# A four-stage layer kernel: first stage built from token rows, head 0 of the delta stage and its out gate reordered, a second weight buffer in the mLSTM stage, weights split inside the branch operand of the last stage

## The chip, the cores and the metric

One core of a Trainium2 chip. The metric is the time of one execution on the device in microseconds (us). Runs of this kernel agree within about 0.2%.

## The reference

One layer for 1,024 prompt tokens and 8 sequences of 8 sample tokens (1,088 tokens, model width 1,024), all in float32.

```python
h = rmsnorm(x, g_mix)
proj = h @ w_in        # q_a k_a v_a i f o_a | qkv_b a_b beta_b z_b | gate_a gate_b
ha = mlstm(q_a, k_a, v_a, i, f) ...            # 4 heads
hb = gated_delta(conv(qkv_b), a_b, beta_b) * silu(z_b)   # 8 heads
mix = sigmoid(gate_a) * (ha @ w_pa) + sigmoid(gate_b) * (hb @ w_pb)
x = x + mix @ w_out
x = x + square(relu(rmsnorm(x, g_ffn) @ w_up)) @ w_down
x = x + sigmoid(rmsnorm(x, g_ple) @ w_pg) * (p @ w_pp)
y = rmsnorm(x, g_final)
```

## The kernel before, in words

Every large product is made exact enough from two rounded parts: an operand is split into a high part (rounded) and a low part (what is left), and a product is three matmuls, low x high, high x low, high x high. A weight slab is 1,024 x 128. SP loads it into a raw buffer, VectorE (DVE) writes its high part (`split_hi`, line 211, tile `w_hi`), GpSimd (POOL) its low part (`split_lo`, line 216, tile `w_lo`), and TensorE (PE) makes 72 matmuls of it: 8 row tiles x 3 matmuls x 3 groups of tokens (384, 384, 320 columns; `product`, line 227). The high and low buffers are double; the raw buffer is single, so the next load waits for `split_lo`. Each engine runs a list written out by hand, with semaphore waits, and there is a barrier between the four stages:

1. `prologue`: loads x by token rows in three pieces, turns it on PE (line 409), squares and sums it over features with a product by ones (line 396), scales it on DVE (line 480), splits it into `hhi` and `hlo` [all 8 row tiles], and stores the turned x (`XT`) to memory.
2. `delta`, tiles `b_*`: first the `gates` part (a product with 24 gate columns of `w_in`, line 616, then a chain of scans and exponentials on DVE and ScalarE (ACT); its rows go to memory as `ROWS_B` and `ROWS_A` and come back to all partitions), woven into the first turn of head 0; then a loop over heads 1 to 6, and head 7. In a turn PE makes the projections K, Q, V, Z of coming heads between the small products of the delta rule. K of the next head is projected in the turn of a head. `out_gate` (line 1581) is DVE's last step of the head before, on what PE turned into two banks (line 1125).
3. `mlstm`, tiles `a_*`: four heads, six slabs each (K, Q, VA, VB, OA, OB), the previous head's output stored to `HA` between the loads of OA and OB on SP's queue. ACT issues loads and stores of the states.
4. `tail`, tiles `t_*`: twice a branch (A, then B): two gate slabs as products with `hhi`/`hlo`, while the branch operand (`HA` or `HB`, 4 loads into `t_rraw`) is split by `branch` into `t_rhi` and `t_rlo`: 8 tiles, high parts and the low parts of odd tiles on DVE, low parts of even tiles on POOL; then the first branch product runs tile by tile (`product_by_tile`, line 239). After that `w_out`, the feed-forward blocks, the last gate and the output.

The order of first use in head 0 is given twice: in the engines' lists (`first_turn`) and in `early`, which assigns PSUM banks.

Of the kernel before, what the change touches and what calls it, by code (L numbers as in the profile page):

```python
# [26 lines left out]
P = 128  # L27
D = 1024
# [217 lines left out]
def build(nc, x_prompt, x_sample, p_prompt, p_sample, state_C, state_n, state_m, state_S, state_conv, g_mix, w_in,  # L246
# [38 lines left out]
    with ctx:  # L285
# [25 lines left out]

        def prologue():
            with ExitStack() as st:
                sb = sbuf_in(st)
                xrow = sb("xrow", [P, NCH, D])
                xT = sb("xT", [P, KT, T])
                sq = [sb(f"sq{i}", [P, KT, 384]) for i in range(2)]
                rb = [sb(f"rb{g}", [P, 384]) for g in range(NG)]
                hf = sb("hf", [P, KT, 384])
                gm = sb("gm", [P, KT])  # L320
                crow = sb("crow", [28, 3 * H_B * P])
                s_x = [sem(f"x_landed{i}") for i in range(3)]
                s_gm, s_small = sem("gm_landed"), sem("small_landed")
                s_const = sem("const_ready")
                s_tr = [sem("x_turned_even"), sem("x_turned_odd")]
                s_cpy = [sem("x_copied_act"), sem("x_copied_dve")]
                s_sq, s_ss, s_ln, s_rs = sem("x_squared"), sem("x_summed"), sem("x_log"), sem("x_rms")
                s_hf, s_hhi, s_hlo = sem("h_made"), sem("h_hi"), sem("h_lo")
                s_out = sem("xT_stored")
                s_ct, s_ctc = sem("conv_turned"), sem("conv_copied")  # L330
                def hf_of(g):

                    return (hf, sq[0], sq[1])[g][:, :, 0:GROUPS[g][1]]

                def turned(eng, half, c, copy):
                    w = L if c < NC else NB * NS
                    eng.wait_ge(s_tr[half], c + 1)
                    src = psum[(2 * c + half) % 6][:].rearrange("p (k t) -> p k t", k=4)[:, :, 0:w]
                    copy(xT[:, 4 * half:4 * half + 4, c * L:c * L + w], src).then_inc(s_cpy[half], 1)

                with nc.Block() as block:
                    @block.sync
                    def _(sp):
# [5 lines left out]
                        sp.dma_start(gm[:], g_mix[0].rearrange("(k p) -> p k", p=P)).then_inc(s_gm, 16)  # L349
                        sp.dma_start(crow[0:24, :], state_conv[0].rearrange("b j c -> (b j) c")).then_inc(s_small, 16)  # L350
                        sp.dma_start(crow[24:28, :], conv_w[0]).then_inc(s_small, 16)
                        sp.wait_ge(s_cpy[0], NCH)
# [5 lines left out]
                    def _(pool):  # L358
# [9 lines left out]
                                           pattern=[[-1, P]], channel_multiplier=1).then_inc(s_const, 1)  # L368
                        pool.affine_select(out=madd[:], in_=madd[:], compare_op=ALU.is_ge, fill=NEG, base=0,
# [13 lines left out]
                        for g in range(2):  # L383
                            a, w = GROUPS[g]
                            pool.wait_ge(s_hhi, g + 1)
                            pool.tensor_tensor(hlo[:, :, a:a + w], hf_of(g), hhi[:, :, a:a + w], ALU.subtract).then_inc(s_hlo, 1)

                    @block.tensor
                    def _(pe):
                        def sums(g):  # L390
                            w = GROUPS[g][1]
                            pe.wait_ge(s_sq, g + 1)
                            if g >= 2:
                                pe.wait_ge(s_ln, g - 1)
                            for k in range(KT):
                                ins = pe.matmul(psum[6 + g % 2][:, 0:w], ones[:], sq[g % 2][:, k, 0:w], start=(k == 0),
                                                stop=(k == KT - 1))
                            ins.then_inc(s_ss, 1)

                        pe.wait_ge(s_const, 7)  # L400
                        for c in range(NCH):
                            w = L if c < NC else NB * NS
                            if c % 3 == 0:
                                pe.wait_ge(s_x[c // 3], 16 if c < 6 else 32)
                            for half in range(2):
                                if c >= 3:
                                    pe.wait_ge(s_cpy[half], c - 2)
                                for k in range(4):
                                    ins = pe.transpose(psum[(2 * c + half) % 6][:, k * P:k * P + w],
                                                       xrow[0:w, c, (4 * half + k) * P:(4 * half + k + 1) * P],  # L410
                                                       ident[0:w, 0:w])
                                ins.then_inc(s_tr[half], 1)
                            if c in (4, 6):
                                sums(c // 2 - 2)
                        sums(2)
# [3 lines left out]
                        for i in range(3 * H_B):  # L419
                            ins = pe.transpose(psum[i // 12][:, 28 * (i % 12):28 * (i % 12) + 28],  # L420
# [5 lines left out]
                    def _(act):  # L426
# [3 lines left out]
                        def squares(g):  # L430
                            a, w = GROUPS[g]
                            act.wait_ge(s_cpy[0], 3 * g + 3)
                            act.wait_ge(s_cpy[1], 3 * g + 3)
                            if g >= 2:
                                act.wait_ge(s_ss, g - 1)
                            act.activation(sq[g % 2][:, :, 0:w], xT[:, :, a:a + w], ACT.Square).then_inc(s_sq, 1)

                        def logs(g):
                            w = GROUPS[g][1]
                            act.wait_ge(s_ss, g + 1)  # L440
                            act.activation(rb[g][:, 0:w], psum[6 + g % 2][:, 0:w], ACT.Ln, scale=1.0 / D, bias=eps[:]).then_inc(s_ln, 1)

                        def exps(g):
                            w = GROUPS[g][1]
                            act.wait_ge(s_ln, g + 1)
                            act.activation(rb[g][:, 0:w], rb[g][:, 0:w], ACT.Exp, scale=-0.5).then_inc(s_rs, 1)

                        def high(g):
                            a, w = GROUPS[g]
                            act.wait_ge(s_hf, KT * (g + 1))  # L450
                            act.activation(hhi[:, :, a:a + w], hf_of(g), ACT.Copy).then_inc(s_hhi, 1)

                        act.wait_ge(s_const, 11)
                        for c in range(3):
                            turned(act, 0, c, copy)
                        squares(0)
                        for c in range(3, 6):
                            turned(act, 0, c, copy)
                        squares(1)
                        logs(0)  # L460
                        exps(0)
                        for c in range(6, NCH):
                            turned(act, 0, c, copy)
                        squares(2)
                        logs(1)
                        logs(2)
                        exps(1)
                        exps(2)
                        for g in range(NG):
                            high(g)  # L470

                    @block.vector
                    def _(dve):
                        def scaled(g):
                            a, w = GROUPS[g]
                            dve.wait_ge(s_rs, g + 1)
                            if g:
# [2487 lines left out]
```

## Time and profile before

| | before |
|---|---|
| median of 3 runs | 2828.61 us (2827.95 to 2834.41) |
| profiled execution, its own time | 2830.69 us |
| its span | 2829.0 us |
| PE, DVE, ACT, POOL busy | 92%, 41%, 23%, 22% |
| mean granted TensorE clock | 0.963 of full speed |

The span runs from the first to the last instruction; the execution's own time is 1.7 us longer. Times in rows are counted from the span's start. Stage 1 lasts to about 68, stage 2 to about 927, stage 3 to about 1383.

### The profile page before, as it was taken

What the parts mean: (1) busy time and instruction counts of PE and PEld (TensorE: products, weight loads), DVE (VectorE), ACT (ScalarE), POOL (GpSimd) and SP (SyncE); (2) the same over time, 40 slices, a digit from 0 to 9 for tenths busy, and PEclk for the clock granted to TensorE, in tenths of its full rate; (3) what the DMA queues carried; (4) which work ended last, traced back from release to release, by engine and by line L of the source; (5) the groups of instructions that cost most, each with busy time, mean ns of one, the idle gap of its engine ahead of it and who ended that gap; (6) DMA issues with size and microseconds to landing.
All of it is one profiled execution on the core that took longest, in us unless ns stands there. A gap on an engine that the chain in (4) does not pass through costs nothing.

```text
span 2829.0 us, 40488 instructions
## 1 busy us (share of the span) xinstructions
PE 2615.4 (92%) x16191; PEld 2542.3 (90%) x16191; DVE 1168.1 (41%) x1930; ACT 645.5 (23%) x1322; POOL 636.1 (22%) x321
## 2 busy tenths in 40 slices
PE   3779999999998799999589999999999999999997
PEld 2769999999997799998489999999999999999897
DVE  4565556556544143453421312654223123134534
ACT  4535454545444111111100000011001000010112
POOL 2332121221210111110122321442212212212421
PEclk7889999999999899999799999999999999999998
DMA  3131221122201316523611211211111111111211
GB/s 131 27 94 43 63 71 54 40 70 63 63 9 31 94 39 95 86 48 53 123 45 44 101 45 44 101 45 45 45 45 45 45 39 52 45 38 45 68 35 67
DMA packets 235322, 165.33 MB, mean 58 GB/s; under 512 B 23211, under 2 KB 222443, under 8 KB 235151
## 3 DMA queue, kind: packets, MB, share of 16 engines
q1 hardware_dynamic: 217414, 154.69, 19.7%
q10 hardware_dynamic: 17792, 8.95, 2.3%
q8 instruction: 90, 1.47, 0.2%
q14 instruction: 26, 0.21, 0.0%
HBM read 135.84 MB, written 27.76 MB: 58 GB/s over the span
## 4 chain that ended last, share of the span: by engine, by line
PE 46%; DVE 2%; issue 1%; DMA 1%; POOL 1%; ACT 0%; POOLq 0%; DVEq 0%; ACTq 0%
PE bank L227 41%; PE bank L239 4%; PE bank L2609 1%; DVE t_rlo L2745 0%; DMA t_w_raw<-in_w_in_dram 0%; PE bank L2646 0%; POOL t_w_lo L216 0%; DVE t_rhi L2742 0%; DVE hlo L2771 0%; DVE hhi L2768 0%; POOL t_rlo L2457 0%; DMA t_rraw<-HB 0%; PE bank L2521 0%; DVE hraw L2915 0%; DVE t_x L2837 0%
## 5 line engine op out<-in xcount | busy, mean ns | idle before, releaser
L216 POOL TENSOR_TENSOR t_w_lo<-t_w_raw,t_w_hi 128x1024 fp32r<-128x1024 f32 x112 | 270.0, 2411 | 953.1 <-DVE t_w_hi L211 953.1
L227 PE MATMUL bank<-t_rlo,t_w_hi 128*128 128x384 f32 (+1 forms) x1248 | 409.5, 328 | 4.6 <-issue 4.6
L227 PE MATMUL bank<-t_rhi,t_w_lo 128*128 128x384 f32 (+1 forms) x1248 | 409.4, 328 | 2.5 <-issue 2.5
L227 PE MATMUL bank<-t_rhi,t_w_hi 128*128 128x384 f32 (+1 forms) x1248 | 409.2, 328 | 0.0
L227 PE MATMUL bank<-hhi,t_w_lo 128*128 128x384 f32 (+1 forms) x1224 | 399.6, 327 | 2.5 <-POOL t_w_lo L216 2.5
L227 PE MATMUL bank<-hhi,t_w_hi 128*128 128x384 f32 (+1 forms) x1224 | 399.7, 327 | 0.0
L227 PE MATMUL bank<-hlo,t_w_hi 128*128 128x384 f32 (+1 forms) x1224 | 399.5, 326 | 0.0
L227 PE MATMUL bank<-hhi,b_w_lo 128*128 128x384 f32 (+1 forms) x768 | 272.1, 354 | 11.4 <-POOL b_w_lo L216 11.4
L227 PE MATMUL bank<-hhi,b_w_hi 128*128 128x384 f32 (+1 forms) x768 | 253.8, 330 | 0.0
L227 PE MATMUL bank<-hlo,b_w_hi 128*128 128x384 f32 (+1 forms) x768 | 253.5, 330 | 0.0
L227 PEld LDWEIGHTS bank<-t_rlo,t_w_hi 128*128 128x128 f32 x1248 | 236.1, 189 | 5.2 <-issue 5.1
L227 PEld LDWEIGHTS bank<-t_rhi,t_w_lo 128*128 128x128 f32 x1248 | 236.0, 189 | 3.1 <-issue 2.9
L227 PEld LDWEIGHTS bank<-t_rhi,t_w_hi 128*128 128x128 f32 x1248 | 236.1, 189 | 0.0
L227 PEld LDWEIGHTS bank<-hhi,t_w_lo 128*128 128x128 f32 x1224 | 230.2, 188 | 3.0 <-POOL t_w_lo L216 3.0
L227 PE MATMUL bank<-hhi,a_w_lo 128*128 128x384 f32 (+1 forms) x576 | 205.5, 357 | 28.2 <-POOL a_w_lo L216 26.7
L227 PEld LDWEIGHTS bank<-hhi,t_w_hi 128*128 128x128 f32 x1224 | 230.2, 188 | 0.0
L227 PEld LDWEIGHTS bank<-hlo,t_w_hi 128*128 128x128 f32 x1224 | 230.1, 188 | 0.0
L2792 DVE TENSOR_TENSOR t_x<-t_x,bank 128x384 f32<-128x384 f32 (+1 forms) x120 | 62.7, 530 | 317.5 <-PE bank L227 276.4
L227 PE MATMUL bank<-hlo,a_w_hi 128*128 128x384 f32 (+1 forms) x576 | 191.9, 333 | 0.0
L227 PE MATMUL bank<-hhi,a_w_hi 128*128 128x384 f32 (+1 forms) x576 | 191.6, 333 | 0.0
L2704 ACT ACTIVATE t_acc<-t_v 128x384 f32<-128x384 f32 (+1 forms) x96 | 48.5, 507 | 614.1 <-DVE t_v L2812 614.1
L211 DVE CAST t_w_hi<-t_w_raw 128x1024 fp32r<-128x1024 f32 x112 | 107.5, 959 | 188.1 <-PE bank L227 132.9
(377 smaller groups left out, 4346.2 us busy)
## 6 DMA issues: line engine op xcount, KB each, us to landing
b_w_raw<-in_w_in_dram SPq DMA_DIRECT2D x32, 512.0 KB, 4.0
t_w_raw<-in_w_up_dram SPq DMA_DIRECT2D x32, 512.0 KB, 3.9
t_w_raw<-in_w_down_dram SPq DMA_DIRECT2D x32, 512.0 KB, 3.9
a_w_raw<-in_w_in_dram SPq DMA_DIRECT2D x24, 512.0 KB
t_w_raw<-in_w_in_dram SPq DMA_DIRECT2D x16, 512.0 KB, 3.7
b_gam<-ROWS_B SPq DMA_DIRECT2D x8, 576.0 KB, 5.0
b_kb<-ROWS_B SPq DMA_DIRECT2D x8, 576.0 KB, 3.6
b_eg<-ROWS_B SPq DMA_DIRECT2D x8, 576.0 KB, 3.5
```

The costliest lines, as they stand in the source:

```text
L211: dve.tensor_copy(self.hi[j % 2][:, 0:kt, :], self.raw[j % self.rs][:, 0:kt, :]).then_inc(self.hi_done, 1)
L216: pool.tensor_tensor(self.lo[j % 2][:, 0:kt, :], self.raw[j % self.rs][:, 0:kt, :], self.hi[j % 2][:, 0:kt, :], ALU.subtract).then_inc(sel ...
L227: ins = pe.matmul(out, a[:, k, :], b[:, k, :], start=(start and k == 0 and i == 0), stop=(stop and k == kt - 1 and i == 2))
L239: ins = pe.matmul(out, x[:, k, :], y[:, k, a:a + w], start=(k == 0 and i == 0), stop=(k == KT - 1 and i == 2))
L2609: ins = pe.matmul(bank[:, 0:w], x[:, k, m * P:m * P + P], v[:, k, a:a + w], start=(k == 0 and i == 0), stop=(k == 1 and i == 2))
L2704: act.activation(ACC[:, a:a + w], V[:, a:a + w], ACT.Square).then_inc(rsq.sem, 1)
L2792: B.release(dve.tensor_tensor(XM[:, m, a:a + w], XM[:, m, a:a + w], src[:, 0:w], ALU.add), ("dense", j, g))
```

## The change

It has six parts.

(1) The first stage works by rows. ACT squares each chunk of 128 tokens, DVE sums it per token, ACT takes the root, DVE the reciprocal, and a diagonal matrix of the reciprocals is the moving operand of a float32 product whose stationary operand is the chunk of x: it turns and scales at once. ACT writes `hhi` from PSUM with the gain as scale, DVE `hlo`. The plain transposes for `XT` stay, between these products.

(2) The gate weights are loaded and split in the first stage. The first load of the delta stage is head 0's K slab, and the memsets for the gate stand in another order.

(3) Head 0: two groups of V stand ahead of the norm of K, Z ahead of K of head 1, and the loads and splits follow.

(4) In the loop `out_gate` stands ahead of the split of the next head's Q.

(5) The mLSTM stage has two raw buffers.

(6) In `branch` the split of the first branch slab stands after four of the eight tiles, on DVE and POOL.

```diff
+                        def scaled(g, k):
+                            n = KT * g + k
+                            if n >= 6:
+                                pe.wait_ge(s_hlo, n - 5)
+                            for i, c in enumerate(chunks_of(g)):
+                                w = rows(c)
+                                if k == 0:
+                                    pe.wait_ge(s_dg, c + 1)
+                                ins = pe.matmul(psum[n % 6][:, L * i:L * i + w], xrow[0:w, c, k * P:k * P + P],
+                                                DG[0:w, c, 0:w], start=True, stop=True)
+                            ins.then_inc(s_h, 1)
...
+                            act.activation(hhi[:, k, a:a + w], psum[n % 6][:, 0:w], ACT.Copy, scale=gm[:, k:k + 1]).then_inc(s_hhi, 1)
...
+                            dve.scalar_tensor_tensor(hlo[:, k, a:a + w], psum[n % 6][:, 0:w], gm[:, k:k + 1],
+                                                     hhi[:, k, a:a + w], ALU.mult, ALU.subtract).then_inc(s_hlo, 1)
...
                 def product(pe):
-                    pe.wait_ge(s_lo, 1)
...
-            early = dense(Q_) + dense(V_) + normed(Q_) + dense(K_)[:1] + thirds("p1") + dense(K_)[1:] + [("rep", 0), ("rep", 1)]
-            early += dense(Z_) + thirds("e0", "kt", "p2", "vt")
+            early = dense(Q_) + dense(V_) + dense(Z_)[:2] + normed(Q_) + thirds("p1") + dense(Z_)[2:] + dense(K_)[:2]
+            early += [("rep", 0), ("rep", 1)] + dense(K_)[2:] + thirds("e0", "kt", "p2", "vt")
...
+                        slab(0, K_, 0, 0)
                         gate.loads(sp)
-                        slab(0, K_, 0, 0)
...
                         slab(0, V_, 2, 0)
+                        slab(0, Z_, 3, 0)
                         gate.stores(sp)
                         for i in (0, 2, 1):
                             row(0, i)
-                        slab(0, K_, 3, 1)
                         sp.wait_ge(gate.done, 1)
                         samples(0)
                         wait(sp, dx, 0, 3)
                         row(1, 0)
                         read(sp, 0, ("p1", 2))
                         row(1, 2)
-                        slab(0, Z_, 4, 0)
+                        slab(0, K_, 4, 1)
                         slab(1, Q_, 1, 1)
...
-                WS = Weights(sb, sem, "a_w", per=NJ)
+                WS = Weights(sb, sem, "a_w", per=NJ, raw_slots=2)
...
-                        def branch(i):
+                        def branch(i, s):
                             for k in range(KT):
+                                if k == KT // 2:
+                                    WS.split_hi(dve, s, 0, B)
                                 if k % 2 == 0:
```

On DVE, in head 0, this stood before around the three thirds of `p1` that `lower` reads (`b_at`), up to the small blocks `b_d` for PE's `replicated` product:

```order
L1519 SCALAR_TENSOR_TENSOR b_dt<-b_gam,b_hg,madds 128x128
L1540 TENSOR_TENSOR b_kb<-b_k,b_kb 128x1152
L1594 TENSOR_TENSOR b_at<-bank,b_dt 128x384 x3
L1530 SCALAR_TENSOR_TENSOR b_cv<-b_xp,b_taps,b_cv 128x1112 x3
L1511 COPY b_taps<-CT 128x84
L1600 TENSOR_TENSOR b_d<-b_at,b_bm 128x1152
```

and this stands there now:

```order
L1565 SCALAR_TENSOR_TENSOR b_dt<-b_gam,b_hg,madds 128x128
L1586 TENSOR_TENSOR b_kb<-b_k,b_kb 128x1152
L211 CAST b_w_hi<-b_w_raw 128x1024
L1640 TENSOR_TENSOR b_at<-bank,b_dt 128x384 x3
L1576 SCALAR_TENSOR_TENSOR b_cv<-b_xp,b_taps,b_cv 128x1112 x3
L1557 COPY b_taps<-CT 128x84
L1646 TENSOR_TENSOR b_d<-b_at,b_bm 128x1152
```

The high part of the fifth slab (K of head 1, whose load stands on SP behind a wait for `p1`) now comes ahead of `lower`.

On DVE in the loop over heads, around `out_gate` (`b_kd<-bank,b_gbh,b_z`), before and then now:

```order
L211 CAST b_w_hi<-b_w_raw 128x1024
L139 REGISTER_ALU
L1581 SCALAR_TENSOR_TENSOR b_kd<-bank,b_gbh,b_z 128x384
L139 REGISTER_ALU
L1581 SCALAR_TENSOR_TENSOR b_kd<-bank,b_gbh,b_z 128x384
```

```order
L1627 SCALAR_TENSOR_TENSOR b_kd<-bank,b_gbh,b_z 128x384
L139 REGISTER_ALU
L1627 SCALAR_TENSOR_TENSOR b_kd<-bank,b_gbh,b_z 128x384
L139 REGISTER_ALU
L1627 SCALAR_TENSOR_TENSOR b_kd<-bank,b_gbh,b_z 128x320
L204 ISA
L139 REGISTER_ALU
L211 CAST b_w_hi<-b_w_raw 128x1024
```

The split went behind the three steps of `out_gate`.

On DVE at the start of the last stage (branch A), now:

```order
L211 CAST t_w_hi<-t_w_raw 128x1024 x2
L2793 CAST t_rhi<-t_rraw 128x1088 x2
L2796 TENSOR_TENSOR t_rlo<-t_rraw,t_rhi 128x1088
L2793 CAST t_rhi<-t_rraw 128x1088 x2
L2796 TENSOR_TENSOR t_rlo<-t_rraw,t_rhi 128x1088
L211 CAST t_w_hi<-t_w_raw 128x1024
L2793 CAST t_rhi<-t_rraw 128x1088 x2
L2796 TENSOR_TENSOR t_rlo<-t_rraw,t_rhi 128x1088
```

Before, the third `t_w_hi` followed the eighth `t_rhi` and the fourth `t_rlo`; POOL's `t_w_lo` moved in the same way.

## Rows read from the trace of the kernel before

**Rows 1.** What PE waited for: us in total, times, longest us.
```profile
PE bank L616 <- DVE gw_lo L677: 33.3, 1, 33.3
PE bank L227 <- POOL a_w_lo L216: 26.7, 4, 14.0
...
PE bank L239 <- POOL t_w_lo L216: 16.4, 3, 9.4
PE bank L227 <- POOL b_w_lo L216: 11.4, 2, 10.8
PE bank L1125 <- DVE b_kd L1581: 10.8, 7, 1.7
...
PE bank L1079 <- ACT b_v L1308: 8.7, 1, 8.7
```

**Rows 2.** Timeline of the first stage: start, us, engine, line, out<-in, count, [idle before <-releaser].
```profile
7.47 6.40 PE L409 MATMUL bank<-ident,xrow 128*128 128x128 f32 x40 [7.47 <-DMA xrow<-in_x_prompt_dram]
...
12.94 2.77 ACT L436 ACTIVATE sq<-xT 128x3072 f32<-128x3072 f32 x1 [0.63 <-DVE xT L339]
...
33.19 0.40 SPq L354 DMA_DIRECT2D XT<-xT  x1
...
68.50 0.10 POOL L588 MEMSET g_bias<- 128x1 f32 x1 [3.50 <-POOLq L262]
...
76.48 0.69 PE L616 MATMUL bank<-hhi,gw_lo 128*128 128x384 f32 x1 [33.27 <-DVE gw_lo L677]
```

**Rows 3.** DMA issues: engine, count, KB each, median us from issue to landing.
```profile
b_w_raw<-in_w_in_dram SPq DMA_DIRECT2D x32, 512.0 KB, 4.0
...
XT<-xT SPq DMA_DIRECT2D x1, 4352.0 KB, 12.3
```

**Rows 4.** Busy time in two stretches: window, us, engines, PEclk, DMA share, GB/s.
```profile
7.50:35.00 27.50, 20.48 (x104) 15.36 (x104) 7.71 (x13) 17.01 (x17) 0.00 (x0) 1.00 0.37 120
1092.60:1099.00 6.40, 6.33 (x27) 6.30 (x28) 0.69 (x1) 0.02 (x1) 1.50 (x1) 0.68 0.76 214
```

**Rows 5.** Timeline of PE: float32 products of 128 columns.
```profile
288.30 2.17 PE L1138 MATMUL bank<-b_q,b_k 128*128 128x128 f32 x18
```

**Rows 6.** Timeline of head 0's first turn, DVE and PE.
```profile
152.08 0.69 DVE L211 CAST b_w_hi<-b_w_raw 128x1024 fp32r<-128x1024 f32 x1 [17.99 <-DMA b_w_raw<-in_w_in_dram]
...
155.24 0.69 PE L227 MATMUL bank<-hhi,b_w_lo 128*128 128x384 f32 x1 [10.75 <-POOL b_w_lo L216]
...
177.85 2.40 PE L1154 MATMUL bank<-b_d,b_bo 128*128 128x512 f32 x4 [5.63 <-DVE b_d L1608]
```

**Rows 7.** Timeline of the loop's first turn, and of head 7.
```profile
280.42 1.77 DVE L211 CAST b_w_hi<-b_w_raw 128x1024 fp32r<-128x1024 f32 x1 [1.69 <-PE bank L227]
...
282.27 2.40 POOL L216 TENSOR_TENSOR b_w_lo<-b_w_raw,b_w_hi 128x1024 fp32r<-128x1024 f32 x1 [0.63 <-DVE b_w_hi L211]
...
322.48 0.42 PE L227 MATMUL bank<-hhi,b_w_lo 128*128 128x384 f32 x1
...
863.22 0.55 PE L1125 MATMUL bank<-ident,b_kbe 128*128 128x128 f32 x3 [0.38 <-DVE b_kd L1581]
```

**Rows 8.** Timeline of the mLSTM stage around head 1's OA slab.
```profile
1063.60 0.60 ACTq L2112 DMA_DIRECT2D out_dram<-a_cs  x1
...
1089.43 0.69 DVE L211 CAST a_w_hi<-a_w_raw 128x1024 fp32r<-128x1024 f32 x1 [12.77 <-DMA a_w_raw<-in_w_in_dram]
```

**Rows 9.** The chain that ended last: start, us, what, count.
```profile
1425.92 14.63 PE bank L239 x72
...
1622.27 13.80 PE bank L239 x72
...
2177.07 12.01 PE bank L239 x72
```

**Rows 10.** Timeline of the last stage's two branch operands.
```profile
1413.20 1.35 DVE L2742 CAST t_rhi<-t_rraw 128x1088 fp32r<-128x1088 f32 x2
...
1622.27 0.65 PE L239 MATMUL bank<-t_rhi,t_w_lo 128*128 128x384 f32 x1 [3.83 <-POOL t_w_lo L216]
```

More of the change, by code:

```diff
@@ L454, in _, with raws @@
+                        def raws(c):
+                            for half in range(2):
+                                if half == 0 or not on_vector(c):
+                                    raw_copy(act, half, c, copy)
+                        act.dma_start(gm[:], g_mix[0].rearrange("(k p) -> p k", p=P)).then_inc(s_gm, 16)
+                        act.wait_ge(s_const, 7)
                         for c in range(3):
-                            turned(act, 0, c, copy)
-                        squares(0)
+                            square(c)
+                            raws(c)
@@ L457, in _ @@
+                        root(0)
                         for c in range(3, 6):
[L458 to L468, printed above, removed]
@@ L469, in _ @@
-                        for g in range(NG):
-                            high(g)
+                            square(c)
+                        act.wait_ge(s_gm, 16)
+                        for g in range(NG):
+                            for k in range(KT):
+                                if g < NG - 1 and k in (2, 4, 6):
+                                    raws(3 * g + 2 + k // 2)
+                                high(g, k)
+                            if g < NG - 1:
+                                root(g + 1)
+                            if g == 0:
+                                for c in range(6, NCH):
+                                    square(c)
+                            if g == 1:
+                                act.wait_ge(s_w, 64)
+                                act.activation(GWH[:], gwr[:], ACT.Copy).then_inc(s_gh, 1)
@@ new lines, in _ @@
+                        raw_copy(dve, 1, 2, dve.tensor_copy)
+                        diagonals(0)
+                        for c in range(3, 6):
+                            reduce(c)
+                        dve.wait_ge(s_gm, 16)
+                        for g in range(NG):
+                            for k in range(KT):
+                                if g < NG - 1 and k == 6:
+                                    raw_copy(dve, 1, 3 * g + 5, dve.tensor_copy)
+                                low(g, k)
+                            if g < NG - 1:
+                                diagonals(g + 1)
+                            if g == 0:
+                                for c in range(6, NCH):
+                                    reduce(c)
@@ L1211, in first_turn @@
                                 whole(0, Q_, g, 0, 1)
+                            for g in range(2):
+                                whole(0, V_, g, 0, 2)
                             pe.wait_ge(s_mask, MASKS)
@@ L1216, in first_turn @@
                                 taken(pe, -1, ("dense", K_, g))
-                            for g in range(NG):
-                                whole(0, V_, g, 0, 2)
+                            whole(0, V_, 2, 0, 2)
                             for g in range(NG):
@@ L1468, in first_turn @@
                             exps(-2, K_)
+                            gate.columns(act)
                             silu(0, Q_, QN)
@@ L1474, in first_turn @@
                                 copy_out(0, V_, g)
-                            gate.columns(act)
                             first_tap(0, 0, V_)
+                            for g in range(2):
+                                z_gate(0, g, False)
                             decays(0)
@@ L1736, in rest @@
                             masks(h)
-                        gate.weights(dve)
                         WS.split_hi(dve, 0, 0, FB)
```

263 lines of the change are left out of this document (134 added, 129 removed).

## The prediction

> **What bounds the kernel now.** I first read the page's busy shares: PE is the engine that is nearly always at work, so the time is PE's work plus PE's waits, and an edit is worth what it takes out of those waits. Next come PE's waits by what ended them [rows 1]: the gate weights of the second stage (33.3 us, once), the mLSTM stage's low weights (26.7 in four, of which 14.0 is that stage's start and stays), the last stage's low weights (16.4 in three), head 0's low weights (11.4) and norm (8.7), and the out gate of the loop (10.8 in seven). Then I read the stretches one by one in the timeline. The first stage hands over at 68.50, and PE stands idle until 76.48 [rows 2], because the second stage begins by zeroing, loading and splitting the gate weights. In head 0 DVE waits 17.99 us for a slab whose load was queued behind the gate rows, and PE waits for that slab and then for DVE [rows 6]. In the loop DVE first waits for PE, then splits, and only then does the out gate [rows 7]. In the mLSTM stage DVE waits 12.77 us for the OA slab to land, which shares the DMA engines with the state stores issued at 1063.60 [rows 8]. In the last stage the wait ends with POOL's low part, which comes after the whole branch operand [rows 10].
>
> A stall costs more than its length: the granted clock falls behind it. In the stretch after the OA wait it averaged 0.68 [rows 4], that is partly 1.2 and partly 2.4 GHz; 72 products took 14.63 and 13.80 after the two branch stalls against 12.01 undisturbed [rows 9].
>
> **The change part by part.**
>
> *Last stage.* Without the stall at branch A, 9.4 [rows 1] and 14.63 - 12.01 = 2.6 [rows 9] go; at branch B 3.83 [rows 10] and 13.80 - 12.01 = 1.8. Sum 17.6. The third wait of that group (16.4 - 9.4 - 3.8 = 3.2) is at the mix operand and stays. Is the slab ready in time? DVE reaches the fifth tile at 1413.20 [rows 10]; the split takes 0.7 (152.08 row [rows 6]) and POOL 2.4 [rows 7], so the low part ends at about 1416.3. PE ends its gate slabs at 1425.92 - 9.4 = 1416.5. That is tight, but a miss would cost only its own length. The operand's later tiles come 0.7 later on DVE and 2.4 later on POOL; PE needs one each 12.01 / 8 = 1.5 us, the eighth at 1427, and DVE has it by about 1424. I take 17.6; the bounds are 12 (a new small wait in each branch) and 17.6.
>
> *mLSTM stage.* Three waits of 26.7 - 14.0 = 12.7 in all [rows 1] are for OA. With two raw buffers its load no longer waits for VB's low part but for VA's, one slab earlier, so it is issued before the state stores at 1063.60 [rows 8] instead of among them. The clock: at a mean of 0.68 over 6.4 us [rows 4], 6.4 x 0.32 = 2.0 is lost; for three about 5. Sum 17.5. What is late next: OB's load now stands behind the two stores to `HA` and is issued while the states are still being written; its split stands on DVE ahead of the steps that free PE's banks. In the old order OA landed at 1089.4 [rows 8] and the bytes in flight are the same, so OB should land near 1091. PE was ready for OA at about 1088 (the split at 1089.43 [rows 8], 0.7 for it and 2.4 on POOL make 1092.5, less a wait of 12.7 / 3 = 4.2), and with OA there it needs DVE for a bank one group later (4.2, a third and a bit of 12.01), at 1092. Bounds: 5 (that wait eats most of it) and 17.5.
>
> *Loop.* Each of six turns loses 1.7 at `out_gate` [rows 1]. Head 7 has no split there and loses 0.38 [rows 7]; that is the same code with the split taken away. The six lose (10.8 - 0.38) / 6 = 1.73 each, so (1.73 - 0.38) x 6 = 8. The split it is moved behind feeds Q of the next head: its low part begins at 282.27, ends at 284.7, and PE uses it at 322.48 [rows 7], so 2 us of delay are covered by 37.8. Bounds 0 and 9.
>
> *Gate wait.* 76.48 - 68.50 = 8.0 [rows 2] becomes about 0.5. But DVE's list has the split of Q ahead of the gate's further steps, and Q's load now waits on K's low part, which waits on POOL's memsets; I count 1 lost. Term 6.5, bounds 5 and 8.
>
> *First stage.* x's first piece lands at 7.5 [rows 2]. Squares of 3,072 columns take 2.77 [rows 2], so a chunk takes 1.0. Three squares, five copies out of PSUM (0.55 each, estimated from that rate), a table load, the root and the diagonals: the first scaled product starts at about 17. A float32 pass of 128 columns costs 2.17 / 18 = 0.12 [rows 5], two passes for a product; per group of 384 tokens PE makes 24 products and 24 transposes, (48 + 24) x 0.12 = 8.7. ACT has eight scaled copies (0.45 each, estimated as above), five plain ones and, in the first group, three squares: 9.5. So each group takes some 9.5, the groups end near 27, 37 and 44, and the split of the gate weights and the copies of the conv columns end at 47. `XT`, issued at 33.19 before [rows 2], is issued at about 36 when the last plain copy is out, and its landing takes 12.3 [rows 3]: 48.5, which ends the stage. With the barrier the next begins at 50 instead of 68.50. Term 18.5. Bounds: 22 (copies faster) and 3 (PE at 1.2 GHz, below). The old work removed (sums, logarithms, the large splits) lay in this stretch and is in the difference of its ends.
>
> The granted clock in this stretch was 1.00 from 7.5 to 35, with PE busy 20.48 of 27.5, on transposes and float32 products mixed [rows 4]. The Trainium skill, page "TensorE: Matmul & The Clock Gate", section "Part 4: PE-mode transpose", says that transposes do not count as PE activity in the way products do; by that the first stage, a third transposes, could run at the low level, and the term would be 3 instead of 18.5. By the row it is 18.5, and I go with the row.
>
> *Head 0.* V's first two groups fill the 8.7 wait of the norm [rows 1], so the gate rows leave earlier, and DVE's wait of 17.99 [rows 6] goes, because Z is loaded ahead of the rows. That moves DVE's tables 18 earlier. Given back: PE now makes two groups of Z ahead of `p1` and waits for Z's weights, +5. Then a new wait: SP loads K of head 1 only after `p1`, with a row ahead of it, and DVE splits it ahead of `lower`: 4.0 of landing [rows 3], some 1.5 for the row and 0.7 for the split, +6.5; behind it on POOL the low part (2.4) stands ahead of the diagonal steps of `b_at`, +1.8. So the replicated product, at 177.85 before [rows 6], gains only 18 - 13.3 = 5. Behind it stood 12.01 of Z [rows 9]; now a third of K remains, and DVE's convolution can follow, which returns about 6. Sum 11; PE's shorter stalls in here bring the low clock into the substitution's small products, and I take 2 off: 9. Bounds 0 and 16.
>
> Edits that I put at nothing: ACT's queue for the gain vector and the memsets' order, hidden behind x's landing and the gate product.
>
> **Sum.** 17.6 + 17.5 + 8 + 6.5 + 18.5 + 9 = 77. The profiled execution took 2830.69, so 2753.6; the median of the runs is 2.1 lower, which makes 2752. About 0.3% is what a measurement of this kernel can tell from no change, 8 us.
>
> **The rivals.**
>
> *The first stage runs at 1.2 GHz.* Passes take 0.24, a group 17, the stage ends near 65: 2752 + 15.5 = 2767. Against it stands the 1.00 of [rows 4]; for it the long wait for x and the serial start. Chance 0.1.
>
> *Head 0 gains nothing.* DVE's wait for K of head 1 and slow small products take all nine: 2761. For it: the load stands behind `p1`. Chance 0.12.
>
> *OB takes OA's place* in the mLSTM stage: if it lands at 1096 or later, DVE holds PE for about 4 in each of three heads: 2764. For it: a store to `HA` ahead in the queue. Chance 0.1.
>
> *Better:* PE keeps 2.4 GHz in head 0 and ACT's copies are quicker: 2738 to 2742. Chance 0.1.
>
> *Slower.* One mechanism could do it: the split moved behind `out_gate` feeds every turn of the loop. It starts to cost when it is more than 37.8 late [rows 7], and to undo 77 us over six turns it would have to be 37.8 + 13 = 51 late in each, with PE idle 13 a turn: 2830 or more. DVE's move is 2. Chance 0.02.
>
> *The change does not do what it says:* PE turns out to be bound elsewhere and the waits reappear one for one, 2825 to 2830. Against it: after each of these stalls PE runs on without another wait for a hundred products or more. Chance 0.02.
>
> **How the numbers follow.** The forecast, 2752, has 0.54. The cases with one rival reach 2767; two together would be 2773. The better case reaches 2738. That range holds 8 in 10 or a bit more. Faster 0.96, same 0.02, slower 0.02.
>
> **What would show it.** Right: the second stage's first instruction near 50, its gate product within 1 of that; no PE wait for OA, and none for the first branch slabs; PE's wait at the out gate below 0.5 in each turn; in head 0 DVE waiting about 10 for the fifth slab ahead of `b_at`. Wrong: a granted clock of 0.5 between 15 and 45; `XT` landing after 55; DVE waiting for OB's landing past 1093 of the old count; Z or K of head 1 holding PE for more than 6.

## The result, and the profile after

The changed kernel takes 2750.96 us (median of 4 runs, 2746.87 to 2752.34), the kernel before 2830.27 beside it (4 runs, 2827.95 to 2834.41): a ratio of 0.9716, 95% interval 0.9699 to 0.9733. The profiled execution took 2750.7, with a span of 2749.0, 80.0 less than before; the mean granted clock is 0.975.

The page's first and third part, busy us (share of the span) and instructions of each engine, before and after, and the queue that brings instructions (packets, MB, share), after:

```profile
PE 2615.4 (92%) x16191; PEld 2542.3 (90%) x16191; DVE 1168.1 (41%) x1930; ACT 645.5 (23%) x1322; POOL 636.1 (22%) x321
...
PE 2610.3 (95%) x16287; PEld 2542.2 (92%) x16287; DVE 1162.0 (42%) x1943; ACT 650.0 (24%) x1352; POOL 622.6 (23%) x320
...
q8 instruction: 89, 1.46, 0.2%
```

PE is busy as long as before: the time came out of its waits. The view of these waits, to be held against [rows 1]:

```profile
PE bank L227 <- POOL b_w_lo L216: 17.6, 2, 13.2
PE bank L227 <- POOL a_w_lo L216: 14.2, 1, 14.2
...
PE bank L239 <- POOL t_w_lo L216: 3.2, 1, 3.2
...
PE bank L1166 <- DVE b_kd L1627: 2.7, 7, 0.4
...
PE bank L662 <- PEq L262: 1.4, 1, 1.4
```

The gate wait is 1.4 where it was 33.3, the mLSTM stage keeps only its start, the last stage only the mix operand, the out gate (now line 1166) 0.4 in each turn. But head 0's weights have grown from 11.4 to 17.6, of which 13.2 in one piece.

The sum was right. Its terms are read from PE's timeline, by the starts of the same instruction in both traces:

| from | before | after | stretch before | after | saved | forecast |
|---|---|---|---|---|---|---|
| start to the first gate product | 0, 76.48 | 0, 57.99 | 76.48 | 57.99 | 18.5 | 25 (18.5 + 6.5) |
| to the out gate's first transpose | 280.22 | 257.84 | 203.7 | 199.9 | 3.9 | 9 |
| to that of head 7 | 862.02 | 831.78 | 581.8 | 573.9 | 7.9 | 8 |
| to the first mLSTM product | 940.77 | 910.19 | 78.8 | 78.4 | 0.3 | 0 |
| to the last stage's first transpose | 1383.72 | 1332.77 | 443.0 | 422.6 | 20.4 | 17.5 |
| to the end of the span | 2829.0 | 2749.0 | 1445.3 | 1416.2 | 29.1 | 17.6 |

Three rows hold within 3 us (the loop, the start of the mLSTM stage and that stage). Two fall short, by 6.5 and 5, and the last stage gives 11.5 more than was forecast. So the number was hit partly because errors cancelled.

The first stage, in the timeline of PE (the third group's products, then the conv columns, then the gate product):

```profile
29.82 1.58 PE L426 MATMUL bank<-dg,xrow 128*128 128x128 f32 x12 [1.82 <-DVE dg L519]
...
36.40 1.60 PE L426 MATMUL bank<-dg,xrow 128*128 128x128 f32 x12
39.86 13.99 PE L426 MATMUL bank<-dg,xrow 128*128 128x128 f32 x48 [1.86 <-DVE dg L519]
53.79 2.76 PE L446 MATMUL bank<-ident,crow 28*128 28x28 f32 x24
57.99 0.66 PE L662 MATMUL bank<-hhi,gw_lo 128*128 128x384 f32 x1 [1.44 <-PEq L262]
```

and busy time in two windows of it (window, length, then PE, PEld, DVE, ACT, POOL, PEclk, DMA share, GB/s):

```profile
28.00:38.00 10.00, 8.18 (x73) 7.83 (x72) 8.96 (x17) 9.26 (x17) 0.00 (x0) 1.00 0.01 2
40.00:54.00 14.00, 14.00 (x50) 11.26 (x51) 3.95 (x8) 3.79 (x8) 0.00 (x0) 0.50 0.68 273
```

The groups were forecast to end near 27, 37 and 44. The first two end at 28 and 38. The third has fewer columns, and no transposes between its products, and takes 14.0 us, at a clock of 0.50; at 1.00 the same 48 passes take 8.07 (e4_k1, below).

Head 0 in POOL's timeline, around the low part of the fifth slab (150.52):

```profile
141.47 1.00 POOL L1052 TENSOR_TENSOR b_at<-b_at,b_off 128x384 f32<-128x384 f32 x1 [19.48 <-DVE b_at L1640]
142.55 1.94 POOL L1054 TENSOR_TENSOR b_at<-b_at,ident 128x384 f32<-128x384 f32 x1
...
149.57 0.99 POOL L1054 TENSOR_TENSOR b_at<-b_at,ident 128x384 f32<-128x384 f32 x1
150.52 2.34 POOL L216 TENSOR_TENSOR b_w_lo<-b_w_raw,b_w_hi 128x1024 fp32r<-128x1024 f32 x1
```

in DVE's:

```profile
140.23 0.69 DVE L211 CAST b_w_hi<-b_w_raw 128x1024 fp32r<-128x1024 f32 x1 [15.36 <-DMA b_w_raw<-in_w_in_dram]
...
142.24 5.45 DVE L1576 SCALAR_TENSOR_TENSOR b_cv<-b_xp,b_taps,b_cv 128x1112 f32<-128x1112 f32 x3
...
150.69 3.38 DVE L1646 TENSOR_TENSOR b_d<-b_at,b_bm 128x1152 f32<-128x1152 f32 x1 [2.73 <-POOL b_at L1054]
```

and in PE's:

```profile
119.37 0.69 PE L227 MATMUL bank<-hhi,b_w_lo 128*128 128x384 f32 x1 [4.45 <-POOL b_w_lo L216]
...
152.91 0.69 PE L227 MATMUL bank<-hhi,b_w_lo 128*128 128x384 f32 x1 [13.19 <-POOL b_w_lo L216]
...
162.92 1.19 PE L1195 MATMUL bank<-b_d,b_bo 128*128 128x512 f32 x4
```

The slab lands at 140.2, but its low part stands behind the six diagonal steps on POOL and is ready at 152.9, and PE waits 13.19 for it. The replicated product comes 162.92 - 57.99 = 104.9 after the gate product, where it came 177.85 - 76.48 = 101.4 after it [rows 2, 6]: 3.5 later, not 5 earlier.

The last stage in the chain that ended last (start, us, what), to be held against [rows 9]:

```profile
1365.32 12.01 PE bank L239 x72
...
1555.22 12.01 PE bank L239 x72
...
2201.94 0.94 issue
2202.87 95.10 PE bank L227 x576
```

Both first branch slabs run without a wait and at 12.01. The chain's last two lines are the place of the surprise: the jump back of PE's loop over feed-forward blocks. The same place in the kernel before:

```profile
2272.09 1.42 issue
2273.51 0.41 PE bank L227
2273.92 2.28 issue
2276.20 97.19 PE bank L227 x575
```

There PE makes one product and stops again ("issue": no wait that the profile shows), and the products behind it take 97.2 instead of 95.1 (the granted clock is 0.82 from 2276.2 to 2290). The second jump, 196 us later, looks alike (1.05 and 2.34). In the changed kernel the second stop is not there.

### The profile page after: what moved, and what is told of

It reads as the page before. It is cut to its first block, busy times and chain, and to the rows that moved or that the text cites. A ratio compares the mean times of both kernels' runs of the same rounds, so it can differ in the third digit from the quotient of the medians.

```text
span 2749.0 us, 40711 instructions
## 1 busy us (share of the span) xinstructions
PE 2610.3 (95%) x16287; PEld 2542.2 (92%) x16287; DVE 1162.0 (42%) x1943; ACT 650.0 (24%) x1352; POOL 622.6 (23%) x320
## 3 DMA queue, kind: packets, MB, share of 16 engines
q8 instruction: 89, 1.46, 0.2%
## 4 chain that ended last, share of the span: by engine, by line
PE 49%; DVE 1%; issue 0%; POOL 0%; ACT 0%; DMA 0%; DVEq 0%; ACTq 0%
PE bank L227 44%; PE bank L239 4%; PE bank L2658 1%; PE bank L2695 0%; DVE hlo L2822 0%; DVE hhi L2819 0%; POOL t_w_lo L216 0%; PE bank L2570 0%; DMA t_w_raw<-in_w_in_dram 0%; DVE hraw L2966 0%; DVE t_x L2888 0%; POOL hlo L2528 0%; DVE hlo L2955 0%; DVE hlo L2953 0%; PE bank L2689 0%
## 5 line engine op out<-in xcount | busy, mean ns | idle before, releaser
L227 PE MATMUL bank<-hhi,b_w_lo 128*128 128x384 f32 (+1 forms) x768 | 271.3, 353 | 18.9 <-POOL b_w_lo L216 17.6
```

Source lines behind the costliest of these rows:

```text
L227: ins = pe.matmul(out, a[:, k, :], b[:, k, :], start=(start and k == 0 and i == 0), stop=(stop and k == kt - 1 and i == 2))
```

## Experiments

"Before" in a ratio is the kernel before on the same chip, whose median there was 2823.27 for e1 to e4, 2831.7 for e5 to e8 and 2830.78 for e9 to e12. The changed kernel itself was measured beside e5 to e8 (e5_after_again) and not beside the others, so a difference from it of a few us is read there from the stretches of the profiles and not from the times.

**e1_three: parts (4) to (6) alone.** On the kernel before: `out_gate` ahead of `split(h + 1, 1, h, K_)`, `raw_slots=2`, and the split inside `branch` as in the diff.

> The kernel before with parts (4), (5) and (6) alone: out gate ahead of the split, two raw buffers in the mLSTM stage, the weight split inside the branch operand. PE's own program is untouched. If the terms of the prediction are right one by one, loop 8, mLSTM 17.5 to 20.4, last stage 17.6 come off: 2830 - 44 = 2786, with the two stalls of 3.7 and 3.4 us at PE's feed-forward loop (2273 and 2470 in the kernel before) still there. Rival: the whole 29 us that the last stage lost in the changed kernel belong to the split; then 2830 - 57 = 2773 and those two stalls are gone.

Measured 2783.81 (2782.36 to 2786.52), ratio 0.9858 (0.9837 to 0.9880). By the same instructions as in the table: loop 574.1 (saved 7.7), mLSTM 420.0 (23.0). Its chain, first branch slabs and feed-forward loop:

```profile
1387.53 12.27 PE bank L239 x72
...
1577.71 12.01 PE bank L239 x72
...
2225.94 1.48 issue
...
2227.83 2.52 issue
2230.36 97.25 PE bank L227 x575
```

By the stretches used below the two branches save 11.5 and 5.6 = 17.1, and the feed-forward stalls are still there: they have nothing to do with part (6). The rival is out, and the terms of the loop and of the branches are right. The mLSTM term depends on the execution it is held against: the time on this chip is 39.5 less, not 44, and 7.7 + 23.0 + 17.1 would be 47.8. e2_shift, which ran here too with one raw buffer, takes 434.1 in the mLSTM stage; against it the stage saves 14.1, and the sum is 38.9.

**e2_shift: PE's program moved.** On the kernel before:

```diff
-                            for i in range(4):
+                            for i in (0, 1, 2, 3) * 2:
                                 ins = pe.transpose(bank[0:27, i * P:i * P + P], CO...[:, 4 * q + i, :], ident[:])
```

> The kernel before, with the 24 small transposes of the convolution columns at the start of the last stage made twice (the same result), so that PE's program is longer ahead of the feed-forward loop and nothing else differs. Theory: the two stalls at that loop's jump back come from where the loop's first instruction falls in the 16 KB pieces in which PE's program is fetched; moved, each shrinks from 3.4 to 3.7 us to about 1 and the low clock behind it goes: 9 us less, 2821. Rival: they come from data or buffers and have nothing to do with the program's place: 2830 to 2833.

Measured 2814.42 (2811.99 to 2822.5), ratio 0.9967 (0.9953 to 0.9981): 8.9 less, with more work on PE. Its chain at the two jumps:

```profile
2264.71 0.96 issue
2265.67 95.09 PE bank L227 x576
...
2455.78 1.30 issue
2457.08 95.10 PE bank L227 x576
```

The second stop is gone at both jumps (e1_three, on the same chip, has it). Theory right: what stands there depends on how much of PE's program lies ahead.

**e7_shift_after and e9_shift32: the stall put back.** On the changed kernel, the same loop over `(0, 1, 2, 3) * (2 if q < 4 else 1)` and over `(0, 1, 2, 3) * (3 if q < 2 else 2)`.

> The changed kernel with 16 of the 24 small transposes at the start of the last stage made twice. By the theory of e2_shift, PE's program ahead of the feed-forward loop is then longer than in the kernel before by 64 float32 products in all, four instructions each with two passes and their weight loads, that is 256 instructions; if one takes 64 bytes that is one whole piece of 16 KB, and the loop's start falls where it fell in the kernel before: the stalls of 3.7 and 3.4 are back and the time is 9 more, 2760. Rival: the place of the program is not it; 2751 to 2752.

Measured 2751.08 (2749.95 to 2754.28): no stall, 1.31 and 1.43 us at the jumps. The count in the expectation was wrong: the trace has one record for a transpose and two for a float32 product.

> The changed kernel with 32 extra small transposes at the start of the last stage. In e7_shift_after a transpose was counted as two passes; the trace has one record for each, so 16 of them are 32 instructions with their weight loads, and the program stood 192 + 32 = 224 instructions behind that of the kernel before. With 32 transposes it is 192 + 64 = 256, one piece of 16 KB at 64 bytes each. Theory: the second stall at the feed-forward loop is back (2.3 us each, and the clock behind it), 9 more, and some 2 for the transposes: 2751 + 11 = 2762. Rival: the place is not it; 2751 to 2754.

Measured 2757.08 (2755.71 to 2762.14), ratio 0.9736 (0.9721 to 0.9751): between the theory and the rival by the time. The last stage of its profiled execution, which took 2762.14, decides: it is 1429.5 instead of 1416.2, and 10.0 of that are at the two jumps. PE's timeline at the two jumps:

```profile
2206.60 0.48 PE L227 MATMUL bank<-t_rhi,t_w_lo 128*128 128x384 f32 x1 [4.20 <-POOL t_w_lo L216]
...
2402.23 0.48 PE L227 MATMUL bank<-t_rhi,t_w_lo 128*128 128x384 f32 x1 [4.29 <-POOL t_w_lo L216]
```

The stall is back, at 4.20 and 4.29, now in one piece ahead of the loop's first product, where the kernel before has 1.42, a product and 2.28; why it is one piece is not shown. (The low part named as releaser ended at 2194.1, 8 us before the jump.) PE's matmul records are 16191 in the kernel before and 16319 here, 128 more, with their weight loads 256 instructions; in e2_shift, the changed kernel and e7_shift_after it is 48, 192 and 224 more, and there the stall is missing. One packet of the instruction queue is 1.46 MB / 89 = 16.4 KB.

**e3_root: no wait between the groups.** On the changed kernel, ACT's `root(g + 1)` and DVE's `diagonals(g + 1)` go from behind a group's eight blocks to ahead of the sixth:

```diff
+                                if g < NG - 1 and k == 5:
+                                    root(g + 1)
                                 high(g, k)
-                            if g < NG - 1:
-                                root(g + 1)
```

> The changed kernel with the root and the diagonals of the next group of tokens moved ahead of the sixth scaled block in the first stage, so that PE does not wait for them between groups (1.82 and 1.86 us). Theory: it is the second of these waits behind which the granted clock fell to 0.50, and the third group's products then took 14.0 us; without it they take 7, the first stage ends with the landing of XT near 50 instead of 57.9, and the time is 2751 - 7 = 2744. Rival: the clock falls there anyway; then only the two waits go, the third group still takes 14, and the time is 2747.

Measured 2744.63 (2743.51 to 2746.21), the theory's number. But the ratio to the kernel before on this chip, 0.9718 (0.9698 to 0.9738), is that of the changed kernel, so the time alone does not show a gain. The profile does: the gate product starts at 52.73, 5.3 earlier (not at 50, since the landing of `XT` ends the stage now), and the third group runs at 1.00.

**e4_k1: head 1's K slab earlier.** On the changed kernel, SP's `slab(0, K_, 4, 1)` goes right behind the rows of head 0, and on POOL `WS.split_lo(pool, 0, 4)` ahead of `unit_lower(0)`.

> The changed kernel with head 1's K slab loaded right behind the rows of head 0 instead of behind the wait for p1, and its low part ahead of the diagonal steps on GpSimd. Theory: PE's 13.2 us wait for that slab's low part goes, and DVE's 15.4 us wait for its landing; the replicated product then waits for DVE's blocks, which come some 6 to 10 us earlier: 2751 - 10 = 2741. Rival: head 0 is bound by the chain of DVE and ACT behind it, and most of the wait comes back ahead of the substitution: gain 4 at most, 2747.

Measured 2735.39 (2731.04 to 2741.39). Head 0's stretch is 187.7 instead of 199.9, some 12 less; PE's wait for the fifth slab is gone, and 6.6 of wait appear ahead of the substitution (it was 2.4). That is more than the theory's 6 to 10 and nearer to the whole 13.2; the rival, 4 at most, is out. But this profile showed something else, in a part of the program that was not touched:

```profile
34.86 1.60 PE L426 MATMUL bank<-dg,xrow 128*128 128x128 f32 x12
38.33 8.07 PE L426 MATMUL bank<-dg,xrow 128*128 128x128 f32 x48 [1.86 <-DVE dg L519]
46.33 1.67 PE L446 MATMUL bank<-ident,crow 28*128 28x28 f32 x24
51.22 0.66 PE L662 MATMUL bank<-hhi,gw_lo 128*128 128x384 f32 x1 [3.22 <-PEq L262]
```

The same wait of 1.86, and then the third group at 1.00, in 8.07 instead of 13.99. The gate product starts at 51.22, within 1 of the forecast.

**e5_after_again: is that chance?**

> The changed kernel as it is, beside the three others on the same chip. Its first stage, alike line for line in e4_k1, took 57.99 us to the gate product in its own profile and 51.22 in that of e4_k1, with the clock at 0.50 in the third group there and 1.00 here. Theory: the clock falls in some executions and not in others, so the runs spread over some 7 us and this profile shows the third group at either 8 or 14 us. Rival: something in e4_k1 decided it, then it is 14 again and 58 to the gate product.

Measured 2750.74 (2744.68 to 2752.32). The third group again at 0.50, the gate product at 57.84. With e7_shift_after, e8_pool_only, e9_shift32 and e10_one_raw there are seven profiles of this first stage: the gate product at 57.99, 57.84, 58.04, 56.50 and 54.87 where the clock fell in the third group, and at 51.22 and 52.50 where it did not. What decides it is not shown. The two in which it did not fall share an edit, GpSimd's low part in head 0, which stands behind this stage; whether that is chance is open too. That a granted clock can differ in this way between two executions of one program is shown by the two profiles of the kernel before (e11_before_again).

**e8_pool_only: the low part where the prediction had it.** On the changed kernel, only `WS.split_lo(pool, 0, 4)` ahead of `unit_lower(0)`.

> The changed kernel with only the low part of head 1's K slab ahead of the diagonal steps on GpSimd, where the prediction took it to stand; its load stays behind p1. Theory: PE's wait of 13.2 shrinks by some 9, since the slab lands at 140 either way, and the diagonal steps come 2.4 later, so the replicated product moves by 4 at most: 2751 - 4 = 2747. Rival: PE's stall is what costs, all 9 come off: 2742.

Measured 2743.19 (2742.15 to 2746.98), which looks like the rival. The profile says otherwise: head 0's stretch is 198.03 instead of 199.85, only 1.8 less, and the rest of its gain is the first stage at 1.00 (gate product at 52.50). PE's waits with a releaser in head 0:

```profile
137.50 0.44 PE L227 MATMUL bank<-hhi,b_w_lo 128*128 128x384 f32 x1 [4.01 <-POOL b_w_lo L216]
151.30 1.44 PE L1196 MATMUL bank<-b_d,b_bo 128*128 128x512 f32 x4 [3.65 <-DVE b_d L1655]
162.79 2.18 PE L1178 MATMUL bank<-ident,b_e 128*128 128x128 f32 x9 [5.09 <-DVE b_e L1676]
```

The wait of 13.2 shrinks by 9.2, as by the theory. Of that come back 3.65 at the replicated product, and 5.09 instead of 2.41 ahead of the substitution. The replicated product itself starts 98.8 after the gate product, 6.1 earlier and not 4 at most, but most of this is waited away behind it. Theory right in place, and the rival is out.

**e10_one_raw: the mLSTM stage undone.** The changed kernel without `raw_slots=2`.

> The changed kernel with one raw buffer in the mLSTM stage, as before. Theory: PE waits for OA again in three heads, 9 to 12.7 in all, and the clock falls behind each; the stage goes back from 422 to between 434 and 443, the time from 2751 to between 2762 and 2771. Rival: part of what the stage gained came from what stands ahead of it in the changed kernel; then it stays under 430 and the time under 2759.

Measured 2765.57 (2759.84 to 2767.68). The stage takes 440.1 instead of 422.6: 17.5, the term of the forecast. In its waits:

```profile
PE bank L227 <- POOL a_w_lo L216: 26.1, 4, 14.1
```

12.0 of them are OA's, beside 12.7 in [rows 1]. Theory right.

**e11_before_again: the kernel before, once more.**

> The kernel before once more, for its sections. Theory: the first stage (76.5), head 0 (203.7), the loop (581.8) and the branches (23.6 and 17.1) repeat within 1 us, while the mLSTM stage, whose OA slab lands among the state stores, differs by several from the 443 of its first profile, as in e2_shift (434), where that part of the program is the same. Rival: it is 443 again, and e2_shift's differs for another reason.

One run, 2833.71. Its stretches: first stage 80.2, head 0 204.6, loop 582.0, mLSTM 440.8, and the feed-forward stalls again (1.11 and 2.25 at the first jump). Head 0, the loop and the branches repeat, within 1 us; the first stage differs by 3.7. The mLSTM stage goes the rival's way, 2.1 from its first profile; the 434.1 of e2_shift was the exception (OA waits of 4.7, 2.8 and 1.2 there), for a reason that is open.

In the first stage the granted clock differs, which is part of the 3.7 at least. The second sixteen of the products by ones take 7.12 here and 5.43 in the first profile, behind the same wait of 2.77. The stretch of [rows 4] and the one behind it, in the first profile (whose row for 7.5 to 35 stands in [rows 4]) and in this one:

```profile
35.00:43.00 8.00, 7.42 (x40) 5.28 (x40) 2.52 (x5) 3.72 (x5) 0.00 (x0) 0.79 1.02 409
...
7.50:35.00 27.50, 22.95 (x104) 16.95 (x104) 5.43 (x8) 15.02 (x16) 0.00 (x0) 0.94 0.33 105
35.00:43.00 8.00, 5.06 (x11) 3.29 (x11) 4.80 (x10) 4.38 (x4) 0.00 (x0) 0.61 0.83 335
```

**e6_best and e12_best_store: a better version.** e6_best is e3_root with e4_k1, and `split(0, 3, 0, Q_)` (head 0's Z) ahead of DVE's `unit(0, K_, KN)`. e12_best_store adds:

```diff
-                        sp.wait_ge(s_cpy[0], NCH)
-                        sp.wait_ge(s_cpy[1], NCH)
-                        sp.dma_start(XT.rearrange("k p t -> p k t"), xT[:]).then_inc(s_out, 16)
-                        sp.wait_ge(s_out, 16)
+                        for n, a, b in ((6, 0, 768), (NCH, 768, T)):
+                            sp.wait_ge(s_cpy[0], n)
+                            sp.wait_ge(s_cpy[1], n)
+                            sp.dma_start(XT[:, :, a:b].rearrange("k p t -> p k t"), xT[:, :, a:b]).then_inc(s_out, 16)
+                        sp.wait_ge(s_out, 32)
```

> The changed kernel with the edits of e3_root and e4_k1 together, and the high part of head 0's Z slab ahead of DVE's norm of K and its convolution of Q instead of behind them. Theory: PE's wait of 4.5 us for Z's low part goes as well; 0 to 7 for the first stage, 12 for head 1's K slab, 4 for Z: 2731 to 2735 where the changed kernel takes 2751. Rival: PE only reaches the norm's replicas or p1 earlier and waits there for DVE instead; then Z gives nothing and the time is that of e4_k1 less the first stage's part, 2735 to 2739.

Measured 2732.06 (2729.68 to 2733.4), ratio 0.9644 (0.9631 to 0.9657). Head 0 is 184.2, 3.5 below e4_k1's 187.7: Z's wait is gone.

> The kernel of e6_best with the store of XT in two pieces, the first 768 tokens as soon as their plain copies are out (near 27) and the rest near 37. In e6_best PE was done with the first stage at 46.9 and waited until 53.1 for the barrier behind the landing of XT. Theory: the rest lands near 42, the stage ends with the conv columns and the gate product starts at 48.5: 2732 - 4.5 = 2727.5. Rival: the store in two pieces is slower, or the gate weights' low part ends later than it: 2730 to 2732.

Measured 2727.34 (2724.34 to 2728.26), ratio 0.9630 (0.9617 to 0.9643). PE's timeline:

```profile
43.70 1.67 PE L447 MATMUL bank<-ident,crow 28*128 28x28 f32 x24
47.78 0.66 PE L663 MATMUL bank<-hhi,gw_lo 128*128 128x384 f32 x1 [2.41 <-PEq L262]
```

With the third group at 1.00 it was the landing of `XT` that ended the stage; taken away, the gate product starts at 47.78, where e6_best had 53.09. This is the fastest kernel of the study.

## Why the prediction was right, step by step

**Last stage.** Right in mechanism and size: from the start of the last product ahead of it to that of its own last product the first branch slab took 24.04 before and 12.01 after, at branch B 17.62 and 12.01: 12.0 + 5.6 = 17.6. No new wait came. What the stage gave beyond that is not this part's. 9.4 come from the two jumps of the feed-forward loop (18.28 and 17.30 from the last product ahead of each to the last of the slab behind it before, 13.01 and 13.15 after), and e2_shift and e9_shift32 show the cause in both directions: the place in PE's program. Part (1) put 96 more passes into it, and by the counts of instructions at which the stall is there or missing the loop's start moved away from the end of a fetched piece; where in a piece it stands no trace shows. The prediction had no such term: it priced what instructions do, and not how many stand ahead of a loop. The Trainium skill, page "Runtime: NRT & Kernel Launch", section "Instruction fetch mechanics", says that instructions are fetched in blocks of 16 KiB, 256 instructions, and that a taken branch to a target outside the current window must wait for a fetch. The runs agree: with 256 more instructions than in the kernel before the stall is back, with 48, 192 and 224 more it is missing.

**mLSTM stage.** Right in mechanism: 17.5 by undoing it, 20.4 between the two profiles, 14.1 on the chip of e1_three and e2_shift, and no wait for OB. How much OA's late landing costs differs between executions. The rival "OB takes OA's place" did not come.

**Loop.** Right: 7.9 of 8, and 0.38 left in every turn, as head 7 had shown.

**Gate wait and first stage.** Together 25 forecast, 18.5 measured. The step that failed: "per group of 384 tokens PE makes 24 products and 24 transposes, 8.7" was taken at a clock of 1.00 for all three groups, because of [rows 4]. It held for the second. The first began at the slow pace (its first twelve passes took 2.93, later ones 1.50) and ended at 28 even so, where 27 was forecast; in the third the clock fell to 0.50 in five of seven profiles, which cost 13.99 - 8.07 = 5.9 in the changed kernel's own. So the rival "the first stage runs at 1.2 GHz" and its sign, a granted clock of 0.5 between 15 and 45, came true for one group of three. The row was weak ground: it is one execution's, it ends where that execution's clock fell (0.79 from 35 to 43), and the second profile of the same kernel reads 0.94 and 0.61 (e11_before_again). In e4_k1, where the third group kept 1.00, the gate product started at 51.22, a gain of 25.3. The wait of 1.86 ahead of that group can't alone be the cause, since the clock also held behind it twice; in the three kernels without it (e3_root, e6_best, e12_best_store) it held each time, which fits but is too few to settle it. The Trainium skill's rule that transposes count for less (page "TensorE: Matmul & The Clock Gate", section "Part 4: PE-mode transpose") does not explain it: the second, mixed, group kept 1.00, and the one without transposes lost it. The trace of the kernel before goes against the rule itself: the 40 float32 transposes that PE makes there first and alone [rows 2] start 0.21 apart up to 11.1 and 0.11 apart from 11.3 on, so the clock rose on transposes alone.

**Head 0.** 9 forecast, 3.9 measured: the step "behind it on POOL the low part stands ahead of the diagonal steps of `b_at`" was wrong. It stands behind them, as the order on POOL would have shown, and PE waits 13.2 for it, which the prediction had listed as a sign of being wrong ("Z or K of head 1 holding PE for more than 6"). DVE's wait for the slab was 15.4 where about 10 was forecast. Behind the replicated product it is as forecast (6): 94.9 instead of 102.4 us to the out gate. Putting the low part where it was thought to be is worth only 1.8 (e8_pool_only); loading the slab earlier as well 12 (e4_k1). So most of the cost came with the load behind `p1`, and the prediction named that as its rival; the earlier load alone was not run.

**The sum.** The first 260 us gave 11.6 less than forecast, the last stage 11.5 more (9.4 of it at the loop's jumps, the rest elsewhere in the stage), the mLSTM stage 2.9 more: 2752 was met at 2750.96 with two terms mis-sized and one missing. That it was met so closely is luck.

## What to carry to other kernels

Check a prediction by stretches and not by its sum: the same instruction's start in both traces shows which terms hold. When a transfer is moved behind a product, look on every engine at what its consumer is queued behind; here the slab's low part stood behind six other steps on GpSimd, and putting it ahead of them paid only once the load came earlier too. And a change that lengthens an engine's program moves every loop behind it: here that alone was worth 9.4 us at two jumps back, and a forecast that prices only what instructions do has no term for it. A granted clock read from one execution is not a constant of the stage: read it in a second one before a term rests on it.

## What the runs showed of the hardware

- A jump back of PE's feed-forward loop cost 0.94 to 1.55 us in ten profiles, and 3.4 to 4.3 in waits in the four others, three with as many instructions on PE ahead of it as the kernel before and one with 256 more. The low clock behind it (0.82 and 0.88 over the next 14 us) nearly doubles the price: 9.4 for two jumps, of which 5.1 are waits.
- The granted clock can differ between executions of the same program in the same place: 5.43 or 7.12 for sixteen products behind the same wait of 2.77, in the two profiles of the kernel before. In kernels alike up to there, 48 passes behind the same wait of 1.86 took 8.07 or 12.6 to 14.1. Runs of one kernel with that wait spread over 4.3 (e7_shift_after) to 10.4 us (e4_k1), those of the three without it over 2.7 to 3.9.
- The column PEclk can't be trusted at the start of a trace: it reads 1.00 from 16.5 to 23 in the changed kernel, where twelve passes took 2.93 us, and 1.50 after 24; in the kernel before it reads 1.00 from 7.5 to 11.3, where transposes start 0.21 apart, and 0.11 behind. Durations tell more.
- DVE and POOL slow each other down: a diagonal step on POOL took 0.99 alone and 1.94 beside DVE's convolution, whose three steps took 5.45 (4.19 elsewhere), and DVE's `b_d` 3.38 beside POOL's low part (1.36 in e4_k1). The Trainium skill, page "SBUF — State Buffer", section "SBUF: two separate sides", says that the two share a pair of ports, which whoever starts first holds for a whole instruction. The rows agree: `b_d` began 0.17 behind the low part and ended at 154.07, 1.21 after the low part's end at 152.86.
